# One more pair of half products in place of two block products, and a reordered tail ahead of the recurrence

## The reference, cut to what matters

```python
h = rmsnorm(x, lp['norm_mix'])
z = h @ lp['w_in']                       # ten column blocks of 256, then 4096 gate columns
qa, ka, va, qb, fb, ib, gb, xc, gc, xd, gl = jnp.split(z, split_at, axis=-1)
k_all, v_all = ka, va                    # branch A: attention; va is an output as well
o_b, S_new = hgrn2(qb, fb, ib, gb, S0, lp)        # branch B: chunked gated recurrence
#   log_f = logaddexp(log(lb), log1p(-lb) + log_sigmoid(fb));  k = (1-lb) sigmoid(-fb)
#   q = silu(qb);  v = ib;  gate silu(gb);  S = exp(b_last) S + (k exp(b_last - b))^T v
gates = jax.nn.sigmoid(gl.reshape(B, L, N_BRANCH, D_MODEL))
x = x + jnp.sum(gates * proj, axis=2) @ lp['w_out']
```

## Time and profile before

| | us |
|---|---|
| median of 3 runs (1749.55 to 1751.46) | 1751.24 |
| profiled execution | 1751.34 |
| its span, first to last instruction | 1749.5 |
| PE busy in it | 1723.3 |
| VectorE / ScalarE / GpSimd busy | 1140.7 / 733.4 / 781.6 |
| mean granted TensorE clock | 0.999 |

### The profile page before, as it was taken

One profiled execution on the slowest core, in us unless ns is written; L12 is line 12 of the kernel. 1 busy time (PEld: TensorE's weight loads), 2 busy tenths in 40 slices (PEclk: granted clock), 3 DMA queues, 4 the chain that ended last, 5 costly groups with the idle time before them and its releaser, 6 DMA issues.

```text
span 1749.5 us, 30931 instructions
## 1 busy us (share of the span) xinstructions
PE 1723.3 (98%) x12865; PEld 1676.3 (96%) x12865; DVE 1140.7 (65%) x1275; ACT 733.4 (42%) x1038; POOL 781.6 (45%) x531
## 2 busy tenths in 40 slices
PE   8999999999999999999999999999999999999998
PEld 8999999998999977899999999999999999999998
DVE  6931115826774667657745877888888887775844
ACT  6433334443422556612335554444444443333521
POOL 1666773431222311212123476677776637668021
PEclk9999999999999999999999999999999999999999
DMA  6643226132221542456524222232222375334032
GB/s 229 76 124 117 99 75 215 37 101 81 67 82 68 196 118 67 159 195 236 209 74 148 86 87 105 101 120 99 99 99 99 117 287 209 117 118 148 26 128 95
DMA packets 84798, 214.80 MB, mean 123 GB/s; under 512 B 14866, under 2 KB 32050, under 8 KB 83506
## 3 DMA queue, kind: packets, MB, share of 16 engines
q1 hardware_dynamic: 73714, 189.48, 31.9%
q0 software_dynamic: 4032, 14.68, 2.7%
q10 hardware_dynamic: 6912, 8.65, 1.4%
HBM read 149.48 MB, written 63.40 MB: 122 GB/s over the span
## 4 chain that ended last, share of the span: by engine, by line
PE 91%; DVE 3%; ACT 2%; DMA 2%; issue 1%; POOL 0%; SPq 0%; DVEq 0%; ACTq 0%; POOLq 0%
PE ps L1656 24%; PE ps L1106 21%; PE ps L1704 10%; PE ps L1093 10%; PE ps L1236 10%; PE ps L1688 3%; PE ps L1324 2%; PE ps L1191 1%; DMA masks<-in_wb 1%; PE ps L1409 1%; PE ps L1133 1%; PE ps L1573 1%; PE ps L1443 1%; PE ps L1430 1%; PE ps L1741 1%
## 5 line engine op out<-in xcount | busy, mean ns | idle before, releaser
L3384 POOL TENSOR_TENSOR Wl<-BIG,Wh 128x512 fp32r<-128x512 f32 x110 | 144.0, 1318 | 115.3 <-ACT Wh L2211 115.3
L3241 POOL CAST Uh<-BIG 128x1024 fp32r<-128x1024 f32 x27 | 36.5, 1350 | 283.8 <-PE ps L1093 193.8
L3030 DVE SCALAR_TENSOR_TENSOR ps<-BIG,fpar,ps 128x1023 f32<-128x1023 f32 x84 | 107.9, 1285 | 36.1 <-ACT ps L2302 35.2
L1093 PE MATMUL ps<-Hh,Uh 128*128 128x352 f32 x384 | 127.2, 331 | 0.8 <-ACT BIG L1940 0.8
L2565 DVE TENSOR_TENSOR BIG<-BIG,ps 128x528 f32<-128x528 f32 x45 | 31.6, 704 | 144.2 <-PE ps L1236 143.9
L1093 PE MATMUL ps<-Hh,Ul 128*128 128x352 f32 x384 | 123.5, 322 | 0.0
L1093 PE MATMUL ps<-Hl,Uh 128*128 128x352 f32 x384 | 123.3, 321 | 0.0
L3336 POOL TENSOR_TENSOR Ul<-BIG,Uh 128x1024 fp32r<-128x1024 f32 x15 | 36.1, 2412 | 163.3 <-ACT Uh L2171 163.3
L1656 PE MATMUL ps<-Hl,Wh 128*128 128x264 f32 x528 | 107.1, 284 | 0.0
L3019 DVE TENSOR_TENSOR BIG<-BIG,ps 128x528 f32<-128x528 f32 x110 | 77.3, 703 | 42.8 <-PE ps L1656 36.9
L1704 PE MATMUL ps<-Sl,Vh 128*128 128x264 f32 x504 | 101.9, 283 | 0.0
(11 more groups left out here) (496 smaller groups left out, 5590.6 us busy)
## 6 DMA issues: line engine op xcount, KB each, us to landing
BIG<-in_wu SPq DMA_DIRECT2D x44, 512.0 KB, 4.6
hidden<-BIG SPq DMA_DIRECT2D x22, 528.0 KB, 2.7
late_gates<-BIG SPq DMA_DIRECT2D x18, 528.0 KB, 3.0
BIG<-sums SPq DMA_DIRECT2D x12, 792.0 KB, 4.9
BIG<-in_wgl SPq DMA_DIRECT2D x9, 1024.0 KB, 6.0
BIG<-in_wd SPq DMA_DIRECT2D x6, 1536.0 KB, 9.7
H<-late_gates SPq DMA_DIRECT2D x17, 528.0 KB, 4.4
gates<-BIG ACTq DMA_DIRECT2D x48, 176.0 KB, 1.9
```

Source lines behind the costliest of these rows:

```text
L1093: ins = nc.tensor.matmul(psb(fill_bank(p)), w[:, u % 2, k], x[:, k, part * PART:part * PART + PART], start=(k == 0 and w is Uh and x is Hh ...
L3030: link(v.scalar_tensor_tensor(y[:, back:SEQ], x[:, 0:SEQ - back], w, y[:, back:SEQ], ALU.mult, ALU.add), v.scalar_tensor_tensor(ys[:, :, b ...
L3384: nc.gpsimd.tensor_tensor(Wl[:, b], src, Wh[:, b].bitcast(F32), ALU.subtract).then_inc(S("w_lo"), 1)
```

## The change

The V columns of z (two tiles) leave the block products and become pair number `Z_PAIR` = 1 of now ten pairs of half products. Their Sigmoid is left out (ACT only counts), and the rows go to `late_gates` in DRAM like a gate's. SP loads them back into `turn` once the transposes of IB0 and of IB1 have read it. In the tail PE has only GB0 and GB1, with groups of transposes inside: two groups behind k-tile 0 of GB0, and two groups of the first V row behind k-tile 4 of GB1. ACT loads the table for Exp and Ln ahead of `before()`, makes the three logarithm steps before it copies GB0, and copies the groups of transposes between the steps of `before()`; GB1 is copied last. Tile numbers and semaphore counts follow.

```diff
-Z_COLS = (1792, 2304, 2048, 1280, 768, 1024, 1536, 512, 256, 0)
+Z_COLS = (1792, 2304, 2048, 1280, 768, 1024, 1536, 256, 0, 512)
-ZB = 14
+ZB = 12
-PAIRS = (4 * LATE - COVER) // 2
+Z_PAIR = 1
+PAIRS = (4 * LATE - COVER) // 2 + 1
-RING = ("XD0", "XD1", "GC0", "GC1", "IB0", "IB1", "QB0", "QB1", "FB0", "FB1", "GB0", "GB1", "VA0", "VA1")
+RING = ("XD0", "XD1", "GC0", "GC1", "IB0", "IB1", "QB0", "QB1", "FB0", "FB1", "GB0", "GB1")
@@ SP
+                first = COVER + 2 * (c - (c > Z_PAIR))
+                src = a["wz"][18:20] if c == Z_PAIR else a["wgl"].rearrange("i v p k m -> (i v) p k m")[first:first + 2]
...
             for i in range(2):
+                sp.wait_ge(*upto(f"g_stored{i}", 16 * (Z_PAIR + 1)))
+                sp.wait_ge(S("vt_done"), 3 * i + 3)
+                sp.dma_start(turn[:, i], late_gates[2 * Z_PAIR + i]).then_inc(on("gw_first") if i else S("cd_in"), 16)
@@ PE
-            turned_v(0, turn[:, 0], range(2))
-            block_z("GB0", (0, lambda: turned_v(0, turn[:, 0], (2,))))
-            turned_v(1, turn[:, 1], range(2))
-            block_z("GB1", (0, lambda: turned_v(1, turn[:, 1], (2,))))
-            block_z("VA0")
-            block_z("VA1")
+            def input_turned():
+                turned_v(0, turn[:, 0], (2,))
+                turned_v(1, turn[:, 1], (0,))
+
+            def values_turned():
+                pe.wait_ge(S("cd_in"), 144)
+                turned_v(2, turn[:, 0], (0, 1))
+            turned_v(0, turn[:, 0], (0, 1))
+            block_z("GB0", {0: input_turned})
+            turned_v(1, turn[:, 1], (1, 2))
+            block_z("GB1", {4: values_turned})
+            turned_v(2, turn[:, 0], (2,))
+            pe.wait_ge(*upto("gw_first", 48))
+            turned_v(3, turn[:, 1])
             for i in range(2):
-                pe.wait_ge(S(f"z_free{i}"), USERS.index(f"VA{i}") // 2 + 1)
-                turned_v(2 + i, turn[:, i])
+                pe.wait_ge(S(f"z_free{i}"), USERS.index(f"GB{i}") // 2 + 1)
             pe.wait_ge(S("vt_free"), 12)
@@ ACT
-            turned_v(0)
-            z_out("GB0", Z[:, GB, :])
-            turned_v(1)
-            z_out("GB1", Z[:, GB + 1, :])
+            turned_out(range(4))
...
             def before():
+                act.preload_act_table_set("natural_log_exp_and_others")
                 act.wait_ge(S("d_rows"), 16)
-                for user in ("FB0", "QB0", "GB0"):
-                    z_wait(user)
-                for user in ("FB1", "QB1", "GB1"):
+                for user in ("FB0", "QB0", "FB1", "QB1"):
                     z_wait(user)
                 link(nc.scalar.activation(bE, f, ACT.Abs))
                 link(nc.scalar.activation(bE, bE, ACT.Exp, scale=-1.0))
                 nc.scalar.activation(bE, bE, ACT.Ln, bias=1.0).then_inc(S("b_acts"), 1)
+                turned_out((4, 5))
+                z_out("GB0", g)
                 act.wait_ge(S("b_pre"), 1)
                 nc.scalar.activation(f, f, ACT.Sigmoid, scale=-1.0).then_inc(S("b_acts"), 1)
                 nc.scalar.activation(bE, q, ACT.Sigmoid).then_inc(S("b_acts"), 1)
+                z_wait("GB0")
                 nc.scalar.activation(bd_, g, ACT.Sigmoid).then_inc(S("b_acts"), 1)
                 act.preload_act_table_set("natural_log_exp_and_others")
+                turned_out((6, 7))
                 act.wait_ge(S("b_pre"), 3)
                 act.wait_ge(S("b_pre"), 2)
                 nc.scalar.activation(bE, b, ACT.Exp).then_inc(S("b_acts"), 1)
                 chunk_decays()
+                turned_out((8, 9))
                 act.wait_ge(S("b_pre"), 5)
                 nc.scalar.activation(bE, bd_, ACT.Exp, scale=-1.0).then_inc(S("b_acts"), 1)
+                turned_out((10, 11))
+                z_out("GB1", Z[:, GB + 1, :])
...
-                    for j in range(2):
-                        z_out(f"VA{j}", turn[:, j])
-                    for j in range(2):
-                        turned_v(2 + j)
```

More of the change, by code:

```diff
@@ L134 @@
          "gc_kept0": ("pages_in3", 0), "gc_kept1": ("s0_in", 0), "a_lo": ("vt_done", 12)}
-PAGES_FROM = (32, 80, 80, 32)
-SIG_FROM = (("pages_in0", 288), ("pages_in1", 336), ("pages_in2", 336), ("pages_in3", 288),
-            ("s0_in", 64), ("cd_in", 128), ("gate_stored0", 384), ("gate_stored1", 384))
+PAGES_FROM = (48, 80, 96, 32)
+SIG_FROM = (("pages_in0", 304), ("pages_in1", 336), ("pages_in2", 352), ("pages_in3", 288),
+            ("s0_in", 64), ("cd_in", 144), ("gate_stored0", 384), ("gate_stored1", 384))
 def made(c, b):
@@ L239 @@
 USERS = ("XC0", "XC1", "XD0", "XD1", "GC0", "GC1", "IB0", "IB1", "C00", "C01", "QB0", "QB1", "C10", "C11", "FB0", "FB1",
-         "D0", "D1", "GB0", "GB1", "VA0", "VA1")
-RING = ("XD0", "XD1", "GC0", "GC1", "IB0", "IB1", "QB0", "QB1", "FB0", "FB1", "GB0", "GB1", "VA0", "VA1")
+         "D0", "D1", "GB0", "GB1")
+RING = ("XD0", "XD1", "GC0", "GC1", "IB0", "IB1", "QB0", "QB1", "FB0", "FB1", "GB0", "GB1")
 FRONT = RING.index("IB1") + 1
@@ L686, in pair_weights @@
             def pair_weights(c, sem):
-                src = a["wgl"].rearrange("i v p k m -> (i v) p k m")[COVER + 2 * c:COVER + 2 * c + 2]
+                first = COVER + 2 * (c - (c > Z_PAIR))
+                src = a["wz"][18:20] if c == Z_PAIR else a["wgl"].rearrange("i v p k m -> (i v) p k m")[first:first + 2]
                 sp.dma_start(gate_raw(c), src.rearrange("h p k m -> p h k m")).then_inc(on(sem), 16)
@@ L787, in _ @@
             for i in range(2):
+                sp.wait_ge(*upto(f"g_stored{i}", 16 * (Z_PAIR + 1)))
+                sp.wait_ge(S("vt_done"), 3 * i + 3)
+                sp.dma_start(turn[:, i], late_gates[2 * Z_PAIR + i]).then_inc(on("gw_first") if i else S("cd_in"), 16)
+            for i in range(2):
                 if i == 0:
@@ L831, in gate_in @@
                 i, u = divmod(s, 8)
-                src = gates[i * EARLY + TURN_OF[u] + QKS] if u < EARLY else late_gates[i * LATE + u - EARLY - COVER]
+                n = i * LATE + u - EARLY - COVER
+                src = gates[i * EARLY + TURN_OF[u] + QKS] if u < EARLY else late_gates[n if n < 2 * Z_PAIR else n + 2]
                 sp.dma_start(gate_row(s), src).then_inc(S(gate_loaded(s)[0]), 16)
@@ L1107, in dense3 @@
                                                    start=(k == 0 and wp == xp), stop=(k == kk - 1 and wp == 1))
-                    if between is not None and k == between[0]:
-                        between[1]()
+                    if between is not None and k in between:
+                        between[k]()
                 return ins
@@ L1621, in _ @@
                 dense3(1 - d % 2, (Ph[:, :, d], Pl[:, :, d]), (chunks(Eh), chunks(El)), KP, None,
-                       (0, last_square) if d == 0 else None).then_inc(S("p_gate"), 1)
+                       {0: last_square} if d == 0 else None).then_inc(S("p_gate"), 1)
             def product(c, b):
@@ L1735, in _ @@
                     dense3(1 - q, (Uh[:, q], Ul[:, q]), normed_x, KD, ("n2_h", 1) if c == 0 else None,
-                           (0, final_sums) if c == 1 else None).then_inc(S("p_gate"), 1)
+                           {0: final_sums} if c == 1 else None).then_inc(S("p_gate"), 1)
                     continue
@@ L1838, in gelu, with turned_out @@
                 nc.scalar.activation(Z[:, GC + i, :], Z[:, GC + i, :], ACT.Gelu_apprx_tanh).then_inc(S("c_gelu"), 1)
-            def turned_v(n):
-                for g in range(3):
-                    m = 3 * n + g
+            def turned_out(ms):
+                for m in ms:
+                    n, g = divmod(m, 3)
                     act.wait_ge(S("vt_done"), m + 1)
@@ L1869, in gate_sig @@
                     act.wait_ge(*upto("g_copied", 2 * c + 2))
-                nc.scalar.activation(GY[:, half], GY[:, half], ACT.Sigmoid).then_inc(on("g_sig"), 1)
+                if c == Z_PAIR:
+                    act.sem_inc(on("g_sig"), 1)
+                else:
+                    nc.scalar.activation(GY[:, half], GY[:, half], ACT.Sigmoid).then_inc(on("g_sig"), 1)
             act.wait_ge(S("zc_done"), 2)
@@ L2613, in _ @@
             scanned(0)
-            dve.wait_ge(*upto("gw_in1", 80))
+            dve.wait_ge(*upto("gw_in1", 96))
             for i in range(2):
```

## The result

The changed kernel took 1755.67 us in the median of 14 runs (1753.97 to 1759.93), the kernel before 1751.68 in 14 runs beside them (1749.55 to 1755.76). The ratio is 1.0021, 95% interval 1.0013 to 1.0029: 4.0 us slower, where 3.4 were forecast. PE's busy time fell by 0.8 us (1723.3 to 1722.5), the span of the profiled execution grew from 1749.5 to 1753.7.

A forecast was written before the change was run, and what follows sets the result against it. PE, 98% busy, was taken as the bound. +20.59 for the pair, -23.29 for two blocks and the gap gave +1.5 for the displaced product, plus 1.9 for the clock: +3.4, so 1754.6 us, range 1749.3 to 1757.

The forecast's parts named there:

- The front: PE's stage of half-product pairs: one pair more, 168 matmuls at 0.1225 us, costs +20.59 us.
- no new wait: PE's front stage: the added pair makes nothing late, so no wait is added to its run.
- The tail on PE and ACT: Block products after D1: 23.29 us of PE work go; PE's transpose groups at 21.3, not ACT, set the next steps.
- The collision: Hand-over after GB1: POOL's cast and subtraction block DVE's sample rows, so the key product ends at 33.5 after D1.
- the displaced product: First recurrence product on PE: starts at 35.6 after D1's end against a break-even of 34.10, +1.5 us.
- Case C: Hand-over: POOL and DVE don't meet, or only in part, 1749.5 to 1750.2 us; chance 0.14.
- The clock: PE's gap of 6.1 us before the turn of keys: granted clock falls to 0.50 for 3 to 7 us, +1.9 us.
- Case B: Hand-over: DVE is blocked but TensorE's clock stays high, 1752.7 us; chance 0.13.
- Case D: Recurrence: low clock through first products and most first fills, 1756.2 us, upper half of A; other new waits 0.06.
- A: The forecast case at the hand-over: DVE blocked and clock falls, 1753.3 to 1757 us; chance 0.62.
- Case E: Whole kernel: PE never waits for more than it did, 1747.5 to 1748.5 us; chance 0.05.
- all waits are as they were, only shifted: Everything behind the first recurrence product: no further gain or loss.

The follow-up runs named there:

- e0: The changed kernel again with no edit: 1756.08 us, ratio 1.0027 against the kernel before.
- e1: The changed kernel with POOL's weight split after GB1 made to wait for the key product: 1753.32 us, ratio 1.0010 against the kernel before.
- e2: The changed kernel with DVE's sample rows moved ahead of the QE product: 1753.96 us, ratio 1.0013 against the kernel before.
- e5: e3 with 12 of the first fill's 24 matmuls moved into PE's hole and two fill blocks' PSUM banks exchanged: 1750.03 us, ratio 0.9989 against the kernel before.
- e10: e5 with the V rows in a DRAM tensor of their own: 1750.05 us, ratio 0.9990 against the kernel before.
- e3: The changed kernel with the edits of e1 and e2 together: 1753.84 us, ratio 1.0021 against the kernel before.
- e4: The changed kernel plus 16 unused matmuls behind PE's last wait, ahead of the turn of the keys: 1754.56 us, ratio 1.0012 against the kernel before.
- e6: The changed kernel plus 33 unused matmuls on PE from the beginning of the hole: 1754.06 us, ratio 1.0018 against the kernel before.
- e9: The changed kernel with the V rows in a DRAM tensor of their own: 1756.09 us, ratio 1.0023 against the kernel before.

## Why the prediction was right, point by point

**The front.** Predicted +20.59, no new wait. The matmuls cost what was said: 1680 in 206.02 us, 0.1226 each. D1's end moved by 370.02 - 349.62 = 20.40, but that this is so close is partly luck. PE's waits in the front, the kernel before and the changed kernel:

```profile
288.45 0.48 PE L1236 MATMUL ps<-Fl,Wh 128*128 128x264 f32 x2 [0.56 <-DVE BIG L2565]
```

```profile
315.71 0.72 PE L1113 MATMUL ps<-Hh,Uh 128*128 128x352 f32 x3 [0.44 <-ACT BIG L1836]
```

The first wait, behind the load of the convolution's rows, comes and goes: it is in the traces of before, e0, e1, e2, e5 and e10 (0.2 to 0.7 us), and not in the others. The second, ahead of QB's first block, is new. It is 0.44 to 0.45 us in every trace of a changed kernel and in none of the three of the kernel before. From the first half product to D1's end the traces without the first wait take 243.4 to 243.5 us before and 264.4 to 264.5 after (the changed kernel, e3, e4, e6, e9), so like with like the front costs 20.9. "No new wait" was wrong by about 0.4 us.

**The tail on PE and ACT.** GB0 ended at 13.03 (predicted 13.07), ACT's copies of the two groups began at 21.33 (21.3), the sample rows at 26.29 (26.4), the key product ended at 33.03 (33.5). One step was wrong, without effect. The logarithms began 8.76 after D1's end and not 7.4, on the landing of D's spill:

```profile
378.78 1.09 ACT L1967 ACTIVATE BIG<-BIG 128x1056 f32<-128x1056 f32 x1 [3.95 <-DMA spill<-BIG]
...
391.35 1.09 ACT L1860 ACTIVATE BIG<-ps 128x512 f32<-128x512 f32 x2 [0.49 <-PE ps L1185]
```

ACT had slack (0.49 us) until PE's groups at 391.35, as the prediction had said, so this cost nothing. The second V row's load made nothing late either.

**The collision.** This was the step that decided the sign, and e1 shows it: 5.33 us of rows against 2.44, with POOL's cast and subtraction under them or not. The prediction had both: a wait for the cast's end, one row, then the subtraction. The size after all offsets, the displaced product, was taken as +1.5; e6 gives +1.16. The first product itself started at 35.95 (predicted 35.6), but for another reason than was written: the key product was 0.5 earlier than predicted, and the turn of the keys ran in the low clock and took 2.78 in place of 2.04. The prediction let the clock be low only behind that point. Case C, no meeting, is out: rows 4 and 7 had shown the block, and the changed kernel (rows) and e2 (key product) have it on both kinds of instruction. The Trainium skill (SBUF — State Buffer, "Who interferes with whom") says that whoever comes second waits for the whole of the other. The trace agrees for DVE: its second row started at 397.39 and ended 0.08 us after POOL's subtraction (399.79 against 399.71). It also agrees the other way round, in the split after GB0, where DVE's scan came first:

```profile
383.62 2.97 DVE L2692 TENSOR_TENSOR_SCAN BIG<-BIG 128x1056 f32<-128x1056 f32 x1
```

```profile
384.46 4.34 POOL L3261 TENSOR_TENSOR Ul<-BIG,Uh 128x1024 fp32r<-128x1024 f32 x1
```

POOL's subtraction took 4.34 us there in place of 2.34; 2.13 of it lie under the scan.

**The clock.** A fall inside the gap, with 3 to 7 us at 0.50, was predicted; 6.8 us were measured. The price was taken as 1.9 from the kernel's start, where the rows show the pace and no granted clock, and e6 against the changed kernel and e0 gives 2.15. The term was right in kind and a little small. That the size comes so close is partly luck, since it hangs on how long the low level lasts and what lies in it: e9 pays 2.67 for the same tail. The Trainium skill (TensorE: Matmul & The Clock Gate, "HAM oscillation — how this bites in real kernels") counts half of the time at the low level as lost; an estimate by it is 3.4 of 6.8. The measured 2.15 is less. The low stretch also holds time in which PE waits (it was busy 5.47 of 6.70 us), and half of the busy time alone is 2.7. Why the rest, 0.6 us, was not lost is not shown.

**The rivals.** Case B (block, clock stays) was refuted: the clock fell in the changed kernel, in e0 and in e9. For it spoke, where PE had work; e1, e2, e3 and e4 show that holes of 2.7, 3.3, 2.3 and 2.3 us end it too. Case D, the low clock through the first products and most of the first fills, did not come: the level rose at 409.27, ahead of the first fill, and the first 48 matmuls of fills took 7.84 us, against 7.89 before. Its price began at 4.5 us of dense work; 5.5 us of PE time were covered, the turn and the products, and the time, 1755.67, lies in the upper half of A, beyond the limit of 1754.7. Case E, the change doing what it wants, is out as long as the hole is there; e5 comes near to what E would have been (1750.03; E had 1747.5 to 1748.5).

**The sum.** Predicted +3.4. In the traces: +20.40 - 20.59 = -0.2 at the front, +1.16 displaced product, +2.25 clock, together +3.2 at the first fill, and +0.9 behind it, which the prediction put at nothing ("all waits are as they were, only shifted"). The medians differ by 4.0. The mechanism was right; the displaced product was taken 0.3 us too large and the clock 0.25 too small. The new wait of 0.44 us ahead of QB was missed, and this pair of traces hides it behind the hole that only the trace of before has. The last 0.9 us were not foreseen and are not explained. So 3.4 comes within 0.6 us of the measured 4.0 partly because small errors of both signs met; the interval of the ratio, 2.3 to 5.1 us, holds both.

## What to carry over

Removing work from the critical engine is not worth the work's own length where it also covered a hand-over. Ahead of removing it, write out when the next product could start without it, with the other engines' work as it will then lie, and look for POOL's casts and subtractions where DVE becomes the last link. If a hole opens on TensorE, its price is the hole and the slow restart together, and real work moved into it from its beginning gives back both (e5 against e3), where work at its end (e4) leaves the hole and the fall.

## What was not expected of the hardware

- Holes of 2.3 to 3.3 us inside dense work were enough for the clock to fall (e1 to e4), and the 2.7 us at the kernel's end are no exception: the level fell as they ended. Counted from where PE became empty, the fall came after 1.9 us in e3, 2.3 in e9, 2.8 in e4, 4.4 in e0 and 4.7 to 4.8 in e1, e2 and the changed kernel. So it could come after PE had taken up work again: 2.05 us into it in e1, 1.5 in e2, 0.5 in e4.
- The low level held for 3.4, 6.8 or 10.2 us in different kernels, and not in the order of the holes: 2.3 us of hole had 6.8 in e3 and 3.4 in e4, 5.6 us had 6.8 in the changed kernel and about as much had 10.2 in e9. In e3 a shorter hole than e1's made the first product later.
- POOL's subtraction got in between two of DVE's rows that follow one another within 0.03 us (DVE's first row ended at 397.36, POOL's subtraction began at 397.37, DVE's second row at 397.39). A run of short instructions on DVE did not hold POOL off. And POOL's cast, with one input, held a row up as its subtraction did (1.05 us in place of 0.3).
- In the changed kernel and in e0 to e4 the clock was high again before the four products of 512 columns, which took 1.91 us in each. In e9 the low level reached 0.45 us into them, and they took 2.15. So what the clock costs hangs on where the low level ends as well.
